# Selection products of a mixture-of-experts tail, moved on TensorE: one ahead of the ninth block's down products, one of the second token tile ahead of the tenth's

## What is computed

```python
def moe_ffn(h, w_router, router_bias, w_gate_l, w_up_l, w_down_l):
    ...
    _, idx = lax.top_k(masked, TOP_K)
    w = jnp.take_along_axis(scores, idx, axis=-1)
    w = w / w.sum(axis=-1, keepdims=True)
    gates = jnp.sum(jax.nn.one_hot(idx, N_EXPERTS, dtype=jnp.float32) * w[..., None], axis=1)
    hid = jax.nn.silu(jnp.einsum('nd,edf->enf', t, w_gate_l)) * jnp.einsum('nd,edf->enf', t, w_up_l)
    hid = hid * gates.T[:, :, None].astype(hid.dtype)
    out = jnp.einsum('enf,efd->nd', hid, w_down_l)
```

## Time and profile before

| what | us |
|---|---|
| time, median of three runs (lowest to highest) | 757.26 (756.87 to 758.19) |
| time of the profiled execution | 757.27 |
| its span, first to last instruction | 755.5 |
| TensorE busy | 723.2 |
| VectorE busy | 328.2 |
| ScalarE busy | 215.8 |
| GpSimd busy | 141.4 |

### The profile page before, as it was taken

How to read it: one execution, slowest core, us unless ns; L and a number is a source line. 1 busy time by engine, 2 the same in 40 slices (tenths; PEclk the granted TensorE clock), 3 DMA queues, 4 the chain that set the end, 5 groups by cost and what they waited for, 6 DMA issues and landing times.

```text
span 755.5 us, 10417 instructions
## 1 busy us (share of the span) xinstructions
PE 723.2 (96%) x3950; PEld 354.8 (47%) x3950; DVE 328.2 (43%) x880; ACT 215.8 (29%) x491; POOL 141.4 (19%) x234
## 2 busy tenths in 40 slices
PE   5899999999999999999999999999999899999995
PEld 3357553346445534433344755435644653443332
DVE  2022625647635552312471253474853556231157
ACT  2210145745024101011322024574602310110132
POOL 4146032220110100101102502313011011010112
PEclk9999999999999999999999999999999999999998
DMA  8999335997208799999896233497430379999962
GB/s 315 354 325 364 113 118 194 386 377 296 113 8 349 305 414 414 423 418 424 315 387 244 92 111 119 164 387 306 175 113 14 126 316 410 422 421 421 423 251 84
DMA packets 65655, 207.95 MB, mean 275 GB/s; under 512 B 8089, under 2 KB 8961, under 8 KB 53315
## 3 DMA queue, kind: packets, MB, share of 16 engines
q1 hardware_dynamic: 54936, 179.86, 61.5%
q10 hardware_dynamic: 5547, 16.12, 5.5%
q0 software_dynamic: 5120, 11.28, 4.4%
HBM read 199.92 MB, written 12.88 MB: 282 GB/s over the span
## 4 chain that ended last, share of the span: by engine, by line
PE 77%; DVE 8%; DMA 8%; ACT 3%; issue 2%; POOL 1%; SPq 1%; POOLq 0%; ACTq 0%; DVEq 0%
PE bank L2413 15%; PE bank L2297 11%; PE bank L2040 8%; PE bank L2428 7%; PE bank L1984 6%; PE bank L2097 5%; PE bank L1905 5%; DMA arena<-in_w_up_dram 3%; PE bank L2026 3%; DMA ring<-in_w_ada_dram 2%; PE bank L2404 2%; PE bank L2142 2%; PE bank L2130 2%; DMA arena<-y_exp,y_idx 2%; PE bank L2389 1%
## 5 line engine op out<-in xcount | busy, mean ns | idle before, releaser
L2413 PE MATMUL bank<-ring,work 128*32 128x512 f32 (+1 forms) x640 | 114.2, 595 | 1.3 <-DMA arena<-in_w_up_dram 1.3
L2413 PEld LDWEIGHTS bank<-ring,work 128*32 128x32 f32 (+1 forms) x640 | 33.3, 120 | 73.1 <-issue 72.0
L1739 DVE COPY xs_tok<-bank 128x256 f32<-128x256 f32 x20 | 8.5, 424 | 134.7 <-PE bank L2420 134.7
L2428 PE MATMUL bank<-ring,xs_tok 128*64 128x512 f32 (+2 forms) x320 | 65.7, 597 | 1.0 <-DVE xs_tok L1739 1.0
L2040 PE MATMUL bank<-arena,ring 128*128 128x384 f32 x192 | 62.2, 486 | 0.0
L2413 PE MATMUL bank<-arena,work 128*64 128x512 f32 (+1 forms) x128 | 56.9, 597 | 0.0
L848 POOL DMA_INDIRECT gather_at<-h_rows,idx x18 | 18.2, 1011 | 173.1 <-PE bank L2404 130.7
L1905 PE MATMUL bank<-ring,cpad 128*32 128x512 f32 x384 | 49.7, 603 | 0.7 <-DMA ring<-in_w_ada_dram 0.7
L2040 PEld LDWEIGHTS bank<-arena,ring 128*128 128x128 f32 x192 | 36.5, 190 | 25.0
L1984 PE MATMUL bank<-ring,arena 128*128 128x512 f32 x96 | 42.8, 598 | 0.9 <-DVE arena L1281 0.6
L2297 PE MATMUL bank<-ring,arena 128*128 128x512 f32 x96 | 43.6, 597 | 0.0
(11 more groups left out here) (384 smaller groups left out, 1100.6 us busy)
## 6 DMA issues: line engine op xcount, KB each, us to landing
ring<-in_w_ada_dram SPq DMA_DIRECT2D x48, 1024.0 KB, 10.1
ring<-in_w_down_dram SPq DMA_DIRECT2D x28, 1024.0 KB, 10.6
ring<-in_w_gate_dram SPq DMA_DIRECT2D x24, 1024.0 KB, 7.2
ring<-in_w_up_dram SPq DMA_DIRECT2D x24, 1024.0 KB, 10.7
ring<-in_w_in_dram SPq DMA_DIRECT2D x15, 1024.0 KB, 14.9
ring<-in_w_out_dram SPq DMA_DIRECT2D x8, 1024.0 KB
arena<-in_w_gate_dram SPq DMA_DIRECT2D x8, 1024.0 KB
arena<-in_w_up_dram SPq DMA_DIRECT2D x8, 1024.0 KB
```

The lines of the kernel that those rows point to most:

```text
L2413: last = mm(bank[b][at:at + n, :].rearrange("p (i f) -> p i f", i=2), rows_T[:, kt * P + at:kt * P + at + n], gate_up_of(s)[:, kt, :, :], ...
L2428: last = mm(bank[5 + hf][at:at + n, :], hidT[:, b, f * P + at:f * P + at + n], w[:, f, hf * 512:(hf + 1) * 512], start=f == 0, stop=f == 1)
```

## The change

One condition and one place in TensorE's list change. The product (0, 0, 1), tile 0, block 7, high half, now stands ahead of the down products of block 8, with the two waits that stood ahead of the first selection product. Ahead of the down products of block 9 stand (0, 0, 0) as before and (1, 0, 0), the first product of tile 1, which is taken out of late_results. This holds in both layers.

```diff
-                            if t == 0 and j == 0:
+                            if (t, j, hf) in ((0, 0, 0), (0, 0, 1), (1, 0, 0)):
                                 continue
...
+                    if b == NB - 2:
+                        pe.wait_ge(s_oh, SELECTIONS * (l + 1))
+                        result_copied(0)
+                        late_product(0, 0, 1)
                     if b == NB - 1:
                         more = rounds_of(pe, l)
-                        pe.wait_ge(s_oh, SELECTIONS * (l + 1))
-                        result_copied(0)
-                        for hf in range(2):
-                            late_product(0, 0, hf)
+                        for t in range(2):
+                            late_product(t, 0, 0)
                     second_half(b)
```

## The result

The changed kernel took 758.72 us, median of 21 runs (757.71 to 761.67), beside 757.69 us for the kernel before, median of 21 (756.70 to 759.44): a ratio of 1.0014, 95% interval 1.0008 to 1.0021. That is 1.03 us slower, or 0.6 to 1.6 us. Programs with these same instructions were timed in four series, 54 runs in all, and their median is 758.26 us against 757.71 us for 147 runs of the kernel before. That is **+0.55 us** (0.3 to 0.9 when the runs of both are drawn again at random). The first series weighs heavily in it: the 33 runs of the three others have a median of 758.06 us, +0.35 us (0.1 to 0.6). The forecast was +0.35 us and a range up to 758.7 us.

The account below looks back on a forecast made before the run. The prediction took VectorE's chain, not TensorE, to bound each layer's tail. It summed 757.27 + 0.27 (layer 1) + 0.08 (layer 0) + 0 (removed product) = 757.62, given as 757.6 us, range 756.4 to 758.7.

Parts of the forecast that it names:

- What bounds the tail: Layer tail: VectorE's chain sets the end, TensorE's selection products run beside it, so the removed product is worth 0.
- The price of a product and the gap: Ahead of block 8's down products: the product takes 0.96 us, the gap hides 0.69, and 0.27 sticks out per layer.
- change of kind: TensorE's switch from a selection product to a down product, priced at 0.10 us; free by the skill's rule.
- the overhang: Part of the product ahead of block 8's down products that the gap does not hide: 0.27 us in each layer.
- Layer 1: Copy of block 9's hidden rows, weighted(0) and the whole VectorE chain in layer 1 move by +0.27 us.
- Layer 0: weighted(0) in layer 0, held by ScalarE's weighting, moves only +0.08 us; bounds 0 and 0.27.
- The time and the range: Whole kernel: 757.6 us, +0.05%, no difference that can be seen; range 756.4 to 758.7 us.
- The tail is TensorE's: Rival: each layer's end moves with TensorE's last product, 0.59 off twice, 756.1 us; chance 0.06.
- hides wholly: Rival: the product ahead of block 8's down products overlaps the copy in full, 757.3 us, even; chance 0.10.
- Does not use the gap: Rival: the product waits until the copy is done, 0.96 on layer 1 and 0.77 on layer 0, 759.0 us; chance 0.05.
- What has room: Work made later but harmless: tile 0's sum, 0.27 later with 1.06 us of room before VectorE reads it.

Follow-up runs that it names:

- the part alone: Kernel before with only (0, 0, 1) ahead of block 8's down products and (1, 0, 0) back in the tail: 758.33 us against 757.62, ratio 1.0010.
- the doubled kernel: Kernel before with (0, 0, 1) and (1, 0, 0) ahead of block 8's down products, (0, 0, 0) alone ahead of block 9's: 759.83 us against 757.70, ratio 1.0025.
- copy of the kernel before: Same instructions in the same order as the kernel before, written through a table: 757.50 us against 757.62, ratio 0.9999.
- three products ahead of block 9: Kernel before with (0, 0, 0), (0, 0, 1) and (1, 0, 0) ahead of block 9's down products, none ahead of block 8's: 758.34 us against 757.62, ratio 1.0013.
- half product: Kernel before plus an overwritten 256-column product ahead of block 8's down products, run twice: 758.05 us against 757.70, then 757.33 against 757.82.
- layer 1 alone: Kernel before with both moves of the change in the second layer only: 758.29 us against 757.75, ratio 1.0008.
- the repeats: Three copies of the changed kernel, same instructions, against the kernel before: 758.13 us against 757.62, 758.12 against 757.70, 757.94 against 757.82.

## Why the prediction was wrong in its size and right in its way

- **What bounds the tail.** Right. VectorE's chain sets the end. One product less in TensorE's tail gave nothing: at the layer's turn TensorE waits the 0.61 away, as forecast, and the part alone, which leaves the tail's product in, is as slow as both (+0.6), with the same intervals in its chain.
- **The price of a product and the gap.** Right: 0.27 from transpose to product and 1.23 to the down products, both as forecast. The 0.10 for the change of kind is there (two products 1.81 in the doubled kernel), as was the overhang that goes with it. The Trainium skill (TensorE: Matmul & The Clock Gate, section "Step-by-step: what each phase is for") has weights loaded ahead of matmuls in flight, where the row groups don't conflict or the load goes to the background weight buffer; were it so at this change of kind, the overhang would be 0.18. The traces show 0.28, and the measurement decides: in the trace before, the first weight load of the down products at block 9 is recorded at 728.62, together with their first matmul and not ahead of it.
- **Layer 1.** Right: forecast +0.27, measured +0.28 between the two copies.
- **Layer 0.** This is the step that failed. "+0.08" took the 0.54 between copy and weighted(0) as room of 0.19 that hides most of the overhang. That room was the late landing of one gather in one execution: ScalarE's weighting waited for it until 3.89 behind block 8's copy (368.45 and 364.56), and 3.18 in the trace of the change. Of the six traces that have no overhang in layer 0 (before, its copy, three products ahead of block 9, the two with the half product, and layer 1 alone), five have 0.34 or 0.35 there, so no room at all. The term is 0.28 in place of 0.08, and the sum 0.56 in place of 0.35. The bound of 0.27 had been written down, with the wrong reason ("if ScalarE's weighting also moved"): it is reached when ScalarE's weighting is simply earlier.
- **The time and the range.** The forecast was 757.62 and the median of 21 runs 758.72, 1.10 more. Of these, 0.42 lie in the start: the forecast began at the profiled execution's 757.27, which was taken to stand at the median from three runs, and the 21 runs of the kernel before have 757.69. Another 0.21 are the term of layer 0 with its rounding. The last 0.47 stay open: no interval of the change's traces shows them, and the repeats did not show them again. The range's upper end was laid by a mechanism thought unlikely. With +0.56 on 757.69, 758.25 was to be expected, and all 54 runs have 758.26; that this fits so well is in part luck, since the repeats alone have 758.06.
- **Rivals.** "The tail is TensorE's" is refuted, and "hides wholly" holds only for the half product. "Does not use the gap" gave 759.0, nearer to the first 758.72 than the forecast, but it did not happen: the product starts before the copy, in all four traces 0.27 or 0.28 behind the transposes.
- **What has room.** Incomplete: tile 0's sum was named and ScalarE's third weighting behind its copy was not. It did not matter to the change and it did to the experiment with three products.

## What to carry to other kernels

A gap in a busy engine's timeline has a size, and a piece of work put into it must be laid against that size with the cost of switching to and fro: here 0.96 against 0.69 lost 0.28 us in each layer, and the half product, an estimated 0.43 + 0.10 = 0.53, lost nothing. First ask who reads what stands behind the gap. Filling the gap paid only once the transposes for which VectorE's chain waits were moved forward too, and moving the transposes alone did not pay either. And a wait that one trace ends with a DMA is no room to count on: count it in several executions, or take it as zero.

## What the runs showed of the hardware that was not expected

- The landing of weights scatters where the DMA engines are busy 90% or more of the time (the page of the kernel before, slices with 414 to 424 GB/s): in layer 0 TensorE waited for block 9's weights between 0.38 us (first half product) and 2.75 us (copy of the kernel before) in programs whose instructions up to there are the same. The spans of the kernel before and of its copy, 755.5 and 758.3, differ by 2.8 us, and this wait alone by 2.3. It is the likely source of the runs' scatter of 756 to 761 us, but beyond this pair that was not tested.
- The switch from selection products to down products costs TensorE 0.09 to 0.10 us beyond the products' own steps (1.81 and 1.82 for two products, 0.96 for one), in the two-product cases though the rows whose weights are to be loaded were ready over a microsecond earlier. Why is not shown.
